# Two layers joined in halves of the tokens, with the squares' sum moved

## The reference

```
def _hybrid_layer(x, ...):            # first layer
    ...
    o = jnp.concatenate([o_mla, o_fox], axis=-1) @ w_out
    return x + _rms_norm(o, g_post)

def second_block(x, w_in, ...):       # second layer
    h = _rmsnorm(x, norm_g[l])
    proj = h @ w_in[l]
    (qa, kca, vca, ksa, vsa, kwa, vwa, za, ga, qb, kb, vb, zb) = jnp.split(proj, offsets, axis=-1)
```

## Time and profile before

| what | value |
| --- | --- |
| median of three runs (1851.46 to 1853.8) | 1853.0 us |
| the profiled execution's own time | 1853.58 us |
| its span | 1851.9 us, mean granted clock 0.994 |
| TensorE busy | 1825.3 us, 99% |
| VectorE busy | 1047.2 us, 57% |
| ScalarE busy | 666.1 us, 36% |
| chain that ended last | TensorE 90%, VectorE 5% |

### The profile page before, as it was taken

How to read it: one execution, slowest core, us unless ns; L and a number is a source line. 1 busy time by engine, 2 the same in 40 slices (tenths; PEclk the granted TensorE clock), 3 DMA queues, 4 the chain that set the end, 5 groups by cost and what they waited for, 6 DMA issues and landing times.

```text
span 1851.9 us, 25540 instructions
## 1 busy us (share of the span) xinstructions
PE 1825.3 (99%) x9062; PEld 1515.8 (82%) x9062; DVE 1047.2 (57%) x1768; ACT 666.1 (36%) x1279; POOL 36.3 (2%) x58
## 2 busy tenths in 40 slices
PE   9999999999999999999999999999999999999998
PEld 7788888888888888778868887888888888888887
DVE  7643434444433787753348954766767666665334
ACT  6532332332223544432226343433433333443222
POOL 0000000000000000000002000000000000000001
PEclk9999999999999999999999999999999999999999
DMA  6322222222232333233238363211212212124332
GB/s 237 102 89 89 79 81 91 83 88 80 86 107 80 125 114 113 91 100 105 91 97 221 103 218 124 69 66 57 69 57 69 91 66 81 57 69 138 123 113 103
DMA packets 54229, 186.16 MB, mean 101 GB/s; under 512 B 6688, under 2 KB 7584, under 8 KB 53664
## 3 DMA queue, kind: packets, MB, share of 16 engines
q1 hardware_dynamic: 49536, 170.78, 27.6%
q0 software_dynamic: 4640, 14.68, 2.9%
HBM read 177.05 MB, written 8.39 MB: 100 GB/s over the span
## 4 chain that ended last, share of the span: by engine, by line
PE 90%; DVE 5%; DVEq 2%; ACT 1%; issue 1%; POOL 0%; ACTq 0%; POOLq 0%
PE strip L421 23%; PE strip L423 23%; PE strip L422 23%; PE scores L421 3%; PE scores L422 3%; PE scores L423 3%; PE outputs L423 2%; PE outputs L422 2%; PE outputs L421 1%; PE scores L476 1%; PE scores L881 1%; PE scores L840 1%; PE scores L909 1%; DVE wl L1447 1%; DVEq L1452 0%
## 5 line engine op out<-in xcount | busy, mean ns | idle before, releaser
L421 PE MATMUL strip<-xh,wh 128*128 128x512 f32 (+1 forms) x1976 | 780.6, 395 | 5.8 <-DVE xl L1838 3.2
L423 PE MATMUL strip<-xh,wl 128*128 128x512 f32 (+1 forms) x1976 | 768.6, 389 | 0.0
L422 PE MATMUL strip<-xl,wh 128*128 128x512 f32 (+1 forms) x1976 | 767.8, 389 | 0.0
L421 PEld LDWEIGHTS strip<-xh,wh 128*128 128x128 f32 x1976 | 372.5, 189 | 82.7 <-DVE xl L1838 4.8
L423 PEld LDWEIGHTS strip<-xh,wl 128*128 128x128 f32 x1976 | 372.2, 188 | 78.1
L422 PEld LDWEIGHTS strip<-xl,wh 128*128 128x128 f32 x1976 | 372.8, 189 | 73.0 <-issue 0.7
L1447 DVE TENSOR_TENSOR wl<-raw,wh 128x1024 fp32r<-128x1024 f32 (+3 forms) x306 | 354.4, 1176 | 119.1 <-ACT wh L993 118.5
L993 ACT ACTIVATE wh<-raw 128x1024 fp32r<-128x1024 f32 (+3 forms) x308 | 306.9, 1022 | 110.0 <-PE strip L423 107.1
L1015 ACT ACTIVATE prob<-scores,nms 128x128 f32<-128x128 f32 (+3 forms) x128 | 66.0, 533 | 129.7 <-DVE nms L1495 129.7
L1255 ACT ACTIVATE e_t<-o 128x512 f32 (+1 forms) x30 | 19.0, 632 | 221.9 <-DVE o L1915 118.1
L421 PE MATMUL scores<-xh,wh 128*128 128x512 f32 (+1 forms) x236 | 89.9, 381 | 0.0
(11 more groups left out here) (434 smaller groups left out, 1878.9 us busy)
## 6 DMA issues: line engine op xcount, KB each, us to landing
raw<-in_w SPq DMA_DIRECT2D x308, 512.0 KB, 3.3
xn<-o POOLq DMA_DIRECT2D x4, 1024.0 KB, 8.3
xr<-xn POOLq DMA_DIRECT2D x16, 256.0 KB, 3.0
o<-in_xt SPq DMA_DIRECT2D x7, 512.0 KB, 8.5
o<-in_xt POOLq DMA_DIRECT2D x14, 256.0 KB, 6.6
out<-oh SPq DMA_DIRECT2D x14, 256.0 KB, 2.5
raw<-in_w SPq DMA_DIRECT2D x2, 256.0 KB, 4.0
o<-in_xt SPq DMA_DIRECT2D x2, 256.0 KB, 4.2
```

Source lines behind the costliest of these rows:

```text
L421: pe.matmul(out, ah, bh, start=first, stop=False, skip_group_check=shared)
L422: pe.matmul(out, ah, bl, start=False, stop=False, skip_group_check=shared)
L423: return pe.matmul(out, al, bh, start=False, stop=last, skip_group_check=shared)
```

## The change

It is confined to the join; elsewhere only counts of semaphores move.

- The last two output strips (14 and 15) are made in halves of 256 tokens: 14 first half, 15 first half, 14 second half (with the first half's token sums after five steps), the first half's spread, 15 second half. Eviction, square, add and root go by halves too. The six copies of the spread product are gone.
- The first six tiles of the second layer's input (`HT`) are scaled, given their residual, split and multiplied by halves: TensorE does tiles 0 to 5 for the first 256 tokens, with the second half's token sums after tile 0 and its spread after tile 2, then tiles 0 to 5 for the other tokens, then tiles 6 to 15 whole.
- The residual transfers of tiles 2 to 5 become two each, of half the size. Scalings run three tiles ahead of low parts instead of four. The stores come after tiles 8, 12 and 15.
- Squares have four buffers instead of two and an accumulator of their own (`acc_mid`, cleared by GpSimd), and their adds come later in VectorE's order: six tiles make 12 half squares, four of them added before tile 6, eight in the iterations of tiles 6 to 9, the whole ones after that. ScalarE's square of tile j waits until its buffer's last content is added.
- The sum of the squares stands ahead of the last strip of the last unit (six products follow it) instead of ahead of the unit.

Helpers not shown: `scale_half`, `rest_half`, `residual`, `xh_half`, `half_square`, `out1_half` on VectorE and ScalarE do for 256 tokens what the whole ones did for 512; `pe_half_sums` is `pe_token_sums` for two of four columns.

```diff
-WARM_FIRST, WARM_MID = 4, 6
+WARM_FIRST = 4
+HT = 6
+X_MID = 3 * KT - 6
+X_OUT2 = 4 * KT - 6 + HT
...
     acc = place("acc", [P, S], offset=at["prob"])
-    sq = [place("sq0", [P, S], offset=at["prob"] + 2048), place("sq1", [P, S], offset=at["prob"] + 4096)]
+    sq = [place("sq0", [P, S], offset=at["prob"] + 2048), place("sq1", [P, S], offset=at["prob"] + 4096),
+          place("sq2", [P, S], offset=at["pth"] + 2048), place("sq3", [P, S], offset=at["pth"] + 4096)]
+    acc_mid = place("acc_mid", [P, S], offset=at["pth"])
...
+    def sq_part(hf, j):
+        n_ = HT * hf + j
+        return sq[n_ // 2 % 4][:, 256 * (n_ % 2):256 * (n_ % 2) + 256]
...
+        g.memset(acc_mid[:, :], 0.0).then_inc(blk_zero, 1)
...
-        for j in range(2, KT):
-            if j >= 6:
-                x_is_added(j - 4)
-            g.wait_ge(scaled, j - 1)
+        for hf in range(2):
+            for j in range(2, HT):
+                if hf:
+                    g.wait_ge(x_added[j % 4], 16)
+                g.wait_ge(scaled, HT * hf + j + 1)
+                g.dma_start(o[:, j, TOKENS[hf]], d["xt"][:, j, TOKENS[hf]], accum_op=ALU.add).then_inc(x_added[j % 4], 16)
+        for j in range(HT, KT):
+            g.wait_ge(x_added[j % 4], 16 * (2 + (j - HT) // 4))
+            g.wait_ge(scaled, HT + j + 1)
             g.dma_start(o[:, j, :], d["xt"][:, j, :], accum_op=ALU.add).then_inc(x_added[j % 4], 16)
-            if j == 7:
-                g.wait_ge(xn_done, 2)
-            if j in (7, 11, 15):
-                xn_store(j - 7)
+            if j == 8:
+                g.wait_ge(xn_done, 4)
+                g.wait_ge(x_added[3], 32)
+                xn_store(0)
+            if j == 12:
+                x_is_added(7)
+                xn_store(4)
+        x_is_added(11)
+        xn_store(8)
...
+    def pe_half_strip(pe, u0, out, hf, steps):
+
+        for k_ in steps:
+            u = u0 + k_ // 8
+            if k_ % 8 == 0:
+                pe.wait_ge(w_lo, u + 1)
+            cols = slice(P * (k_ % 8), P * (k_ % 8) + P)
+            ins = three(pe, out[:, 0:256], wh[u % SLOTS][:, cols], wl[u % SLOTS][:, cols], xh[:, k_, TOKENS[hf]],
+                        xl[:, k_, TOKENS[hf]], k_ == 0, k_ == KT - 1)
+            if hf == 1 and k_ % 8 == 7:
+                ins.then_inc(w_used, 1)
+        if hf == 0 and k_ == KT - 1:
+            ins.then_inc(part_done, 1)
...
+        for hf in range(2):
+            for j in range(HT):
+                pe.wait_ge(x_lo, X_MID + HT * hf + j + 1)
+                if hf == 0 and j % 2 == 0:
+                    pe.wait_ge(w_lo, u0 + j // 2 + 1)
+                for s in range(4):
+                    ins = tile(j, s, TOKENS[hf], hf == 0 and j == 0, False)
+                if hf == 1 and j % 2 == 1:
+                    ins.then_inc(w_used, 1)
+                if hf == 0:
+                    aside(j)
+        for u in range(HT // 2, 8):
+            steps = [(2 * u + a, s) for a in range(2) for s in range(4)]
+            if u == 7:
+                steps = [(2 * u + a, s) for s in range(4) for a in range(2)]
+            for j, s in steps:
+                if s == 0:
+                    pe.wait_ge(x_lo, X_MID + HT + j + 1)
+                    pe.wait_ge(w_lo, u0 + u + 1)
+                ins = tile(j, s, slice(0, S), False, j == KT - 1)
+                if j == KT - 1 and s < 3:
+                    ins.then_inc(four_done, 1)
+                if j == KT - 1 and s == 2:
+                    pe.wait_ge(sq_used, KT + HT + KT)
+                    pe.matmul(px[:, :], ones[:, :], acc_mid[:, :], start=True, stop=True).then_inc(sum_done, 1)
+            ins.then_inc(w_used, 1)
...
-        with pe.Fori(1, KT // 2 - 1) as i:
+        with pe.Fori(1, KT // 2 - 2) as i:
             for s in range(4):
                 half(pe, At(U_OUT1 + 4 + s, i, 4), N_OUT1 + s // 2, s % 2, N_OUT1 + 1 + s // 2 + i * 2)
-        pe_token_sums(pe, 3, N_OUT1 + KT)
-        pe_spread(pe, 0, (po,))
-        for i in range(WARM_MID):
-            pe.matmul(px[:, :], ones[:, :], gate[:, :], start=True, stop=True)
-        pe_four(pe, U_CMPIN, 3 * KT - 6, sb, summed=(4, 7))
+
+        def out1_half(hf, j, steps):
+
+            if steps[0] == 0:
+                if hf == 0:
+                    pe.wait_ge(y_done, N_OUT1 + 13 + j)
+                else:
+                    pe.wait_ge(half_out, j + 1)
+            pe_half_strip(pe, U_CMPIN - 4 + 2 * j, pj[(N_OUT1 + j) % 2], hf, steps)
+
+        out1_half(0, 0, range(KT))
+        out1_half(0, 1, range(KT))
+        out1_half(1, 0, range(5))
+        pe_half_sums(pe, 0, 3, (half_sq, 2))
+        out1_half(1, 0, range(5, KT))
+        pe.wait_ge(diag_done, 2)
+        pe.matmul(po[:, 0:256], ones[:, :], gate[:, 0:256], start=True, stop=True).then_inc(spread, 1)
+        out1_half(1, 1, range(KT))
+
+        def aside(j):
+
+            if j == 0:
+                pe_half_sums(pe, 1, 4, (ev_act, N_OUT1 + KT))
+            if j == 2:
+                pe.wait_ge(diag_done, NQ)
+                pe.matmul(px[:, :], ones[:, :], gate[:, :], start=True, stop=True).then_inc(spread, 1)
+
+        pe_mid(pe, U_CMPIN, sb, aside)
...
+        def sq_half(hf, j):
+            if HT * hf + j >= 8:
+                a.wait_ge(sq_used, KT + HT * hf + j - 7)
+            a.activation(sq_part(hf, j), o[:, j, TOKENS[hf]], ACT.Square).then_inc(sq_done, 1)
+
+        half_square(0, 0)
+        half_square(0, 1)
+        act_root(a, 3, 0, 2)
+        half_square(1, 0)
+        act_hi(a, At(U_CMPIN))
+        xh_half(0, 0)
+        xh_half(0, 1)
+        act_hi(a, At(U_CMPIN + 1))
+        xh_half(0, 2)
+        xh_half(0, 3)
+        sq_half(0, 0)
+        sq_half(0, 1)
+        half_square(1, 1)
         act_hi(a, At(U_CMPIN + 2))
+        act_root(a, 4, 2, 4)
+        xh_half(0, 4)
+        xh_half(0, 5)
+        sq_half(0, 2)
         act_hi(a, At(U_CMPIN + 3))
-        act_root(a, 3)
-
-        for j in range(KT):
-            if j < 2:
-                a.wait_ge(xn_done, j + 1)
-            else:
-                a.wait_ge(x_added[j % 4], 16 * (j // 4 + (j % 4 >= 2)))
+        for j in range(3, HT):
+            sq_half(0, j)
+        xh_half(1, 0)
+        xh_half(1, 1)
+        for j in range(2, HT):
+            sq_half(1, j - 2)
+            xh_half(1, j)
+            if j == 3:
+                act_hi(a, At(U_CMPIN + 4))
+        act_hi(a, At(U_CMPIN + 5))
+        sq_half(1, 4)
+        sq_half(1, 5)
+        for j in range(HT, KT):
+            a.wait_ge(x_added[j % 4], 16 * (3 + (j - HT) // 4))
             a.activation(xh[:, j, :], o[:, j, :], ACT.Copy, scale=c("g_2", j)).then_inc(x_hi, 1)
-            if j >= 2:
-                a.wait_ge(sq_used, KT + j - 1)
-            a.activation(sq[j % 2][:, :], o[:, j, :], ACT.Square).then_inc(sq_done, 1)
-            if j in (5, 7, 9, 11):
-                act_hi(a, At(U_CMPIN + (j + 3) // 2))
+            a.wait_ge(sq_used, KT + 2 * j - 6 if j < 9 else KT + HT + j - 3)
+            a.activation(sq[j % 4][:, :], o[:, j, :], ACT.Square).then_inc(sq_done, 1)
+            if j in (8, 10):
+                act_hi(a, At(U_CMPIN + j // 2 + 2))
         act_hi(a, At(U_CMPIN + 8))
-        act_rms(a, 4)
+        act_rms(a, 5)
...
+        out1_half(0, 0)
+        half_add(0)
+        out1_half(0, 1)
+        token_rms(v_, 3, 0, 2)
+        def residual(hf, j):
...
+        out1_half(1, 0)
+        v_.wait_ge(spread, 1)
+        scale_half(0, 0)
+        scale_half(0, 1)
+        v_.wait_ge(xr1_in, 16)
+        residual(0, 0)
+        half_add(1)
+        v_.drain().then_inc(r_done, 1)
+        scale_half(0, 2)
+        residual(0, 1)
+        for j in range(3, HT):
+            scale_half(0, j)
+        rest_half(0, 0)
+        lo(v_, At(U_CMPIN))
+        rest_half(0, 1)
+        lo(v_, At(U_CMPIN + 1))
+        rest_half(0, 2)
+        out1_half(1, 1)
+        v_.drain().then_inc(r_done, 1)
+        rest_half(0, 3)
+        token_rms(v_, 4, 2, 4)
         lo(v_, At(U_CMPIN + 2))
+        rest_half(0, 4)
+        rest_half(0, 5)
+        v_.wait_ge(spread, 2)
+        scale_half(1, 0)
+        scale_half(1, 1)
+        residual(1, 0)
+        scale_half(1, 2)
+        residual(1, 1)
+        scale_half(1, 3)
+        rest_half(1, 0)
+        scale_half(1, 4)
+        scale_half(1, 5)
+        rest_half(1, 1)
         lo(v_, At(U_CMPIN + 3))
-        v_.wait_ge(spread, 1)
-
-        def scale_tile(j):
-            ins = v_.scalar_tensor_tensor(o[:, j, :], o[:, j, :], c("g_post", j), po[:, :], ALU.mult, ALU.mult)
-            if j >= 2:
-                ins.then_inc(scaled, 1)
-
-        def residual(j):
-            v_.drain()
-            v_.tensor_tensor(o[:, j, :], o[:, j, :], xr1[:, j, :], ALU.add).then_inc(xn_done, 1)
-
-        scale_tile(0)
-        v_.wait_ge(xr1_in, 16)
-        residual(0)
-        scale_tile(2)
-        scale_tile(1)
-        x_rest(0, o[:, 0, :], c("g_2", 0), 3 * KT - 6)
-        residual(1)
-        scale_tile(3)
```

(44 more changed lines are left out.)

132 lines of the change are left out of this document (87 added, 45 removed).

## The result

The changed kernel takes 1860.7 us in the median (1859.18 to 1863.46), the kernel before, beside it, 1852.98 (1851.46 to 1853.8). The ratio is 1.0045, with a 95% interval from 1.0033 to 1.0057: 7.7 us slower. 1861 was forecast, with a range from 1853 to 1868.

The account below looks back on a forecast made before the run. TensorE, busy 99% of the span, was taken as the bound. Third strip 5.9 us later plus 1.7 for the clock gave +7.6 on the median 1853.0: 1860.6, rounded 1861; range 1853 to 1868.

Parts of the forecast that it names:

- The join: Between the two layers: the second layer's first product starts at 960.35, 10.8 us earlier than before.
- Half transfers: Residual transfers of 128 KB for the second layer's first tiles: 1.0 us apart, 4.1 to land, the first at 961.3.
- or if the half transfers' readers wait longer than 4.1: Listed sign of a wrong prediction: readers of the 128 KB residual transfers wait longer than 4.1 us.
- Tiles 6 to 15: Second layer's whole input tiles: 30.0 us from tile 6's low part to tile 15's; TensorE's last unit 7.9 us late.
- VectorE's own work and transfers set the sum at 1011.5: Tiles 6 to 15, if squares and copies slip past each other less tightly: squares' sum at 1011.5, +1.8 us.
- the ring: Tiles 6 to 15: squares wait for buffers' adds, copies behind squares; 3.1 us a tile against TensorE's 2.72.
- second rival: Tiles 6 to 15: square buffers don't bind; +1.8 us, and +1.7 if the clock falls: 1856.5; chance 15%.
- The sum: Squares' sum in the last unit: issued at 1015.7, 4.1 us behind the unit's start at 1011.6.
- The chain: From squares' sum to third strip behind the first block: 27.9 us, so the strip starts at 1043.6, 5.9 us later.
- The clock: At the third strip behind the first block: granted clock falls to half after 2.5 us of idleness, costing 1.7 us.

## Why the prediction was right, point by point

Times of the profiled execution of after are put on the clock of before by adding 0.58.

- **The join.** The first product was forecast at 960.35 and came at 960.50. Half scaling 0.48, half low part 0.48, drained half add 0.43 to 0.5, half copy 0.51: the durations taken from the earlier trace rows hold. The half copy of 0.50, for which there was no row, was right to 0.01. By the formula of the Trainium skill (ScalarE: Activation LUTs, What ACT_TABLE_LOAD costs) it is 0.49, and the trace agrees: 0.49 to 0.51.
- **Half transfers.** The first was issued at 956.85 and read at 960.09: 3.2 us, not 4.1. Hence the wait before the second sums of 0.91 and not 1.8. But the fourth, issued at 958.85, was read only at 966.47, and the fourth of the second group (971.97) at 979.62, after a wait of 2.95 us: 7.6 us each, and not 1.0 apart. By the prediction's own list ("or if the half transfers' readers wait longer than 4.1") this is a sign of being wrong, and it was: TensorE waits 1.91 us ahead of the last half tile, just before tile 6, where 0.6 was forecast. The low part of tile 6 starts at 982.92 instead of 981.1. The estimate of 2.3 us by the Trainium skill (DMA: Bandwidth & Descriptors, Anatomy of one DMA) was too low for the first, and far too low for the fourth. The page of the kernel before had a warning: of its 14 accumulating transfers the median took 6.6 us to land, and I had read only the first (4.7).
- **Tiles 6 to 15.** Forecast were squares idle 1.9 to 3.5 us, TensorE's waits of 6 to 8 us, the longest before tile 11, and 30.0 us from the low part of tile 6 to that of tile 15. Measured: 1.85 to 3.40 for tiles 6 to 11 (tile 12's square didn't wait, tile 13's 1.01), 6.1 for TensorE (and the 1.9 just before tile 6), 2.55 before tile 11, and 31.2. The rows came nearly as forecast, and yet the step "VectorE's own work and transfers set the sum at 1011.5" if the ring doesn't bind, on which my second rival's price rested, is wrong. With the ring gone the sum stood at +68.5, where it had stood, and not 4.2 us earlier. What failed is that I treated the transfers' lead as given: I didn't follow the stores of 1024 KB that the change puts between the transfers of tiles 8 and 9, and 12 and 13. With both gone the 4.3 us are there.
- **The sum.** Forecast 1015.7, measured 1018.5; in the two other kernels with the same code up to it +68.2 and +68.6, which is 1017.3 and 1017.7. So the sum was 1.6 to 2.8 us later than forecast. 1.0 to 1.8 of it stood there at tile 6 already, behind the late fourth transfer; that it comes from there is read from the rows alone, no run took it away. The granted clock fell among these tiles too, which the prediction didn't count: at 980.7 behind the wait of 1.91 us in the changed kernel's profile, and behind the wait of some 2.55 before tile 11 in those of the two others. What that cost at the sum isn't shown; waits follow each fall, and the profile with the earliest of the three has the latest sum.
- **The chain.** 27.9 forecast, 27.93 measured, and 27.94 in the kernel before with the sum late. The wait of some 1.5 us ahead of the second of these strips came too (1.37). This step carries the result, and that run shows it by itself.
- **The clock.** 1.7 us were counted for one fall behind the third strip. It fell there in four of the seven profiles with that wait and no filling. But behind the third strip the kernel before has a fall in its profile too, at 1131.9, and with fewer copies it has none there. How much of this term the medians hold isn't shown, and there is little room for it. The third strip of the two kernels just named would be at +68.2 or +68.6 plus 27.9, so at +96.1 to +96.5, 7.4 to 7.8 us later than +88.7, and that alone is the median's 7.7. So, as far as the profiles tell, the total was right by luck, with two errors that cancel: the sum some 2 us too early, and most of the 1.7 us for the clock too much.

## What to carry to other kernels

A wait that one sees in the trace is not yet the limit: take it away and look at who waits next at the same place. Here two limits of equal height, buffers that come free late and transfers queued behind stores, each made the other's removal worthless. Before a gain at a join is counted, find the next fixed chain behind it (here 27.9 us from the sum on) and ask when its first instruction can be issued; a lead of 11 us ahead of that instruction was worth nothing, and a cheap edit that moved that instruction by 1.5 us, two idle products fewer, gave 2.6 us where the whole rebuilding lost 7.7. When two profiles are compared, place the falls of the clock first and measure between marks that neither kernel touches.

## What the runs showed of the hardware

- The granted clock fell to half for some 3.4 us behind short idle times of TensorE in some executions and not in others, in code that is the same: behind 2.03 to 2.10 us near 60 us in 10 of the 14 profiles, behind 2.24 to 2.29 near 773 in 8, behind 2.22 near 1129 to 1141 in 7, and behind 2.53 to 2.57 before tile 11 in three of four kernels with the same code up to there. A fall behind the third strip or near 1131 to 1141 cost 1.6 us.
- Four accumulating transfers of 128 KB issued one behind the other had their readers 3.2 us (first) and 7.6 us (fourth) behind their own issue, in both groups, not at even steps.
- An accumulating transfer of 256 KB with no store ahead of it (the kernel with squares and stores moved) took 4.2 to 5.4 us from issue to reader for six of the eight tiles from 8 to 15, and 6.6 and 6.9 for the other two. Right behind a store of 1024 KB it took 7.65 and 8.80 us (squares moved alone).
